# Which engine compares the token numbers in the expert stage of a hybrid decoder step

## The reference

```
pg = softmax(x @ w_rg); g_top = argmax(pg); pg_top = max(pg)          # 4 groups
fl = (x @ w_re) of the 4 experts in group g_top; pf = softmax(fl)
top_p, top_i = top_k(pf, 2)
wts = top_p / sum(top_p) * pg_top;  eid = g_top * 4 + top_i           # 16 experts
act = silu(h @ w_gate[e]) * (h @ w_up[e])                             # 2048 -> 512
y   = sum over the two chosen e of wts * (act @ w_down[e])            # 512 -> 2048
x   = x + y;   result = RMSNorm(x)
```

## Time and profile before

| what | us |
|---|---|
| median of 3 runs | 1614.38 |
| lowest and highest of them | 1611.1 and 1617.32 |
| the profiled execution, its own time | 1609.06 |
| its span, from the first to the last instruction | 1607.3 |
| TensorE busy | 1386.7 (86%) |
| VectorE busy | 682.8 (42%) |
| GpSimd busy | 247.9 (15%) |
| mean granted TensorE clock | 0.931 |

### The profile page before, as it was taken

One profiled execution on the slowest core, in us unless ns is written; L12 is line 12 of the kernel. 1 busy time (PEld: TensorE's weight loads), 2 busy tenths in 40 slices (PEclk: granted clock), 3 DMA queues, 4 the chain that ended last, 5 costly groups with the idle time before them and its releaser, 6 DMA issues. The chain is left out here.

```text
span 1607.3 us, 27516 instructions
## 1 busy us (share of the span) xinstructions
PE 1386.7 (86%) x10524; PEld 857.5 (53%) x10524; DVE 682.8 (42%) x1199; ACT 330.3 (21%) x734; POOL 247.9 (15%) x176
## 2 busy tenths in 40 slices
PE   7999999998999798778999899587889878887554
PEld 4478887777888566544544664433334333333221
DVE  3154333433553455574100223525455545654225
ACT  3001001222433244474000222111011111111102
POOL 0000000003000000000000000055344534453230
PEclk9999999999998699798999999789899989998877
DMA  9244547434430477104932234788958899859995
GB/s 346 104 171 168 188 146 259 149 120 171 172 112 7 144 233 233 47 1 172 310 111 105 96 114 187 298 321 367 377 245 326 353 421 375 367 191 418 421 422 217
DMA packets 108676, 360.96 MB, mean 225 GB/s; under 512 B 16462, under 2 KB 44150, under 8 KB 80290
## 3 DMA queue, kind: packets, MB, share of 16 engines
q1 hardware_dynamic: 104866, 329.63, 53.9%
q0 software_dynamic: 3232, 22.16, 3.8%
q10 hardware_dynamic: 512, 8.26, 1.4%
HBM read 482.68 MB, written 17.05 MB: 311 GB/s over the span
## 5 line engine op out<-in xcount | busy, mean ns | idle before, releaser
L2509 PE MATMUL bank<-ring,hT_e 128*32 128x256 f32 x3328 | 220.2, 415 | 87.6 <-DMA ring<-in_w_exp_up 50.1
L2597 DVE TENSOR_TENSOR x<-x,bank 128x1024 f32<-128x1024 f32 x156 | 183.1, 1215 | 262.8 <-PE bank L2496 256.7
L2465 POOL COPY ring<-ring 128x2048 f32 x104 | 194.9, 1902 | 246.8 <-DMA ring<-in_w_exp_gate 236.8
L2509 PEld LDWEIGHTS bank<-ring,hT_e 128*32 128x32 f32 x3328 | 113.2, 117 | 217.9 <-issue 168.9
L1853 PE MATMUL bank<-W,mixT 128*128 128x512 f32 x256 | 112.7, 600 | 1.6 <-DVE mixT L2088 1.6
L2525 PE MATMUL bank<-W,const 128*32 128x512 f32 x832 | 95.8, 596 | 13.1 <-ACT const L2555 11.2
L2496 PE MATMUL bank<-const,own_rows 32*128 32x512 f32 (+1 forms) x600 | 92.2, 685 | 6.7 <-DVE x L2597 6.7
L1853 PEld LDWEIGHTS bank<-W,mixT 128*128 128x128 f32 x256 | 48.9, 193 | 63.0 <-issue 60.8
L2551 ACT ACTIVATE gate<-bank 64x256 f32<-64x256 f32 x26 | 9.8, 376 | 321.9 <-PE bank L2509 321.9
L1833 POOL MEMSET mix<- 128x1024 f32 x1 | 1.0, 952 | 453.9 <-PE bank L1845 453.9
L517 PE MATMUL bank<-raw,hT 128*128 128x256 f32 (+1 forms) x288 | 65.2, 384 | 0.0
(11 more groups left out here) (424 smaller groups left out, 2069.7 us busy)
## 6 DMA issues: line engine op xcount, KB each, us to landing
ring<-in_w_exp_gate SPq DMA_DIRECT2D x108, 1024.0 KB
ring<-in_w_exp_up SPq DMA_DIRECT2D x104, 1024.0 KB
W<-in_w_exp_down SPq DMA_DIRECT2D x104, 1024.0 KB
raw<-in_w_in SPq DMA_DIRECT2D x10, 2048.0 KB
raw<-in_w_in SPq DMA_DIRECT2D x8, 2096.0 KB
W<-in_w_out SPq DMA_DIRECT2D x3, 4096.0 KB, 13.5
k_in<-in_cache_sel_k SPq DMA_DIRECT2D x64, 128.0 KB, 2.3
v_in<-in_cache_sel_v SPq DMA_DIRECT2D x64, 128.0 KB, 3.4
```

The costliest lines, as they stand in the source:

```text
L2465: pool.tensor_copy(w_g[:, quarter(q), :], held[:, quarter(q), :]).then_inc(g_copied[q], 1)
L2509: mm = pe.matmul(GATE[lane, 0:256], hT[:, k, q, :], (w_g if n < 2 else w_u)[:, c, cols], start=(c == 0), stop=(c == KC - 1))
L2597: ins = dve.tensor_tensor(x[rows, r, cols], x[rows, r, cols], src[rows, :], ALU.add)
```

## The change

GpSimd makes `own_rows` instead of VectorE. `find_rows` moves to GpSimd's loop, behind the gather and ahead of the copy of gate quarter 2 (the third). It is now two instructions: a copy of the unit's column of `token_of` into a new one-column tile `row_token`, and the comparison with that column. A semaphore (`token_picked`) stands between them. Ahead of them GpSimd waits until the moves of the unit before are done (`moved`); that count starts at 3, so the waits of VectorE's `add` are raised by 3. A further semaphore (`token_ready`) tells GpSimd once that the token numbers are written. After the loop the last two units are written out: quarters 0 and 1, `find_rows`, quarters 2 and 3, `find_rows`. TensorE's code stays.

```diff
--- before.py
+++ after.py
@@ -2376,6 +2376,7 @@
             hT = side("hT_e", [P, 4, 4, UNIT])
             gate = side("gate", [P, FF // 2])
             from_row = side("from_row", [P, 1], I32)
+            row_token = side("row_token", [P, 1])
             token_no = side("token_no", [P, UNITS_EACH, UNIT])
             own_rows = side("own_rows", [P, TOK])
             UP = slice(P // 2, P)
@@ -2387,7 +2388,7 @@
                 sem("e_" + n) for n in ("pe_passed", "slot_ready", "h_turned", "h_copied", "silu_ready", "act_ready", "a_turned", "a_copied",
                                         "y_copied"))
             gathered = sem("e_gathered")
-            own_ready, moved, added, own_moved, summed = (sem("e_" + n) for n in ("own_ready", "moved", "added", "own_moved", "summed"))
+            own_ready, token_ready, token_picked, moved, added, own_moved, summed = (sem("e_" + n) for n in ("own_ready", "token_ready", "token_picked", "moved", "added", "own_moved", "summed"))
             junk = w_d[:, 0, :]
             ms = side("f_ms", [P, TILES])
             squared, scaled, rooted, ready, stored = (sem("f_" + n) for n in ("squared", "scaled", "rooted", "ready", "stored"))
@@ -2464,19 +2465,35 @@
                                 pool.wait_ge(gu_used[q], turn)
                             pool.tensor_copy(w_g[:, quarter(q), :], held[:, quarter(q), :]).then_inc(g_copied[q], 1)
 
+                    def find_rows(turn):
+                        pool.tensor_copy(row_token[:, :], token_of[:, bass.ds(turn, 1)]).then_inc(token_picked, 1)
+                        pool.wait_ge(token_picked, turn + 1)
+                        pool.sem_inc(pool_passed, 1)
+                        pool.tensor_scalar(own_rows[:, :], token_no[:, :, :].rearrange("p k j -> p (k j)"), row_token[:, 0:1], None,
+                                           ALU.is_equal).then_inc(own_ready, 1)
+
                     expert_of = lambda turn: pool.value_load(experts[0:1, bass.ds(turn, 1)], min_val=0, max_val=NE - 1)
                     before_last = count(pool, 2)
                     gather(0)
                     copy_gate(0, range(4), expert_of(0), later=False)
                     pool.wait_ge(h_turned, 1)
                     gather(1)
+                    pool.wait_ge(token_ready, 1)
+                    pool.sem_inc(moved, 3)
                     with pool.Fori(0, before_last) as turn:
                         e = expert_of(turn + 1)
                         copy_gate(turn + 1, (0, 1), e)
                         pool.wait_ge(h_turned, turn + 2)
                         gather(turn + 2)
+                        pool.wait_ge(moved, turn * 3 + 3)
+                        find_rows(turn)
                         copy_gate(turn + 1, (2, 3), e)
-                    copy_gate(before_last + 1, range(4), expert_of(before_last + 1))
+                    copy_gate(before_last + 1, (0, 1), expert_of(before_last + 1))
+                    pool.wait_ge(moved, before_last * 3 + 3)
+                    find_rows(before_last)
+                    copy_gate(before_last + 1, (2, 3), expert_of(before_last + 1))
+                    pool.wait_ge(moved, before_last * 3 + 6)
+                    find_rows(before_last + 1)
 
                 @block.tensor
                 def _(pe):
@@ -2586,10 +2603,6 @@
                                                  scalar=row_w[UP, bass.ds(turn, 1)], in1=gate[UP, :],
                                                  op0=ALU.mult, op1=ALU.mult).then_inc(act_ready, 1)
 
-                    def find_rows(turn):
-                        dve.tensor_scalar(own_rows[:, :], token_no[:, :, :].rearrange("p k j -> p (k j)"), token_of[:, bass.ds(turn, 1)], None,
-                                          ALU.is_equal).then_inc(own_ready, 1)
-
                     def add_tile(r, banks):
                         rows = slice(0, TILE_ROWS[r])
                         for h, src in enumerate(banks):
@@ -2598,16 +2611,16 @@
                         return ins
 
                     def add(turn, r):
-                        dve.wait_ge(moved, turn * 3 + r + 1)
+                        dve.wait_ge(moved, turn * 3 + r + 4)
                         add_tile(r, bank2[0:2]).then_inc(added, 1)
 
                     dve.tensor_copy(token_no[:, 0, :], cst("slot_no")[:, 0:UNIT])
                     own.link(dve.tensor_tensor(token_no[:, 1:, :], cst("slot_no")[:, 0:UNIT].unsqueeze(1).to_broadcast([P, UNITS_EACH - 1, UNIT]),
                                                cst("tile_over")[:, 1:].unsqueeze(2).to_broadcast([P, UNITS_EACH - 1, UNIT]), ALU.add))
                     dve.sem_inc(added, 3)
+                    dve.sem_inc(token_ready, 1)
                     drain(0)
                     activate(0)
-                    find_rows(0)
                     drain(1)
                     add(0, 0)
                     add(0, 1)
@@ -2615,13 +2628,11 @@
                     with dve.Fori(1, last) as turn:
                         activate(turn)
                         add(turn - 1, 2)
-                        find_rows(turn)
                         drain(turn + 1)
                         add(turn, 0)
                         add(turn, 1)
                     activate(last)
                     add(last - 1, 2)
-                    find_rows(last)
 
                     def add_last(k):
                         dve.wait_ge(own_moved, k + 1)
```

## The result

The changed kernel takes 1634.38 us at the median of 4 runs (1631.17 to 1638.5), the kernel before on the same chip 1614.49. The ratio is 1.0125, with a 95% interval from 1.0095 to 1.0156: slower by 20 us. The forecast of 1618 was too low, and the time lies 4 us above the range. The profiled execution took 1631.17 us (span 1629.4, mean granted clock 0.924). L2472 is now the comparison on GpSimd, L2513 the move, L2526 gate and up, L2542 the down projection.

The account below looks back on a forecast made before the run. Expert stage: weight loads bound its end from 1437, set by when loads after 1435 begin. Load order +0.6, unit 19's clock +1.1 and five experts' clock +1.6 made +3.3 us on the 1614.38 median: 1618, range 1608 to 1630.

Parts of the forecast that it names:

- the margin of the loads: In five experts before unit 19, the last up load could come 3.6 us later free; excess 0.9, counted as +1.6 us.
- Rival 2: Each new wait breaks the load chain: +9.7 us, 1624; decided by quarters freed over 3.6 us later; chance 0.23.
- The new wait: In an expert's second units TensorE waits for GpSimd's comparison behind the next gate landing: 2.5 to 4.4 us, eight times.
- The clock: After such waits TensorE falls to half clock in seven of ten cases, 1.6 us each: +1.1 at unit 19, +1.6 before.
- The comparison on GpSimd: Added per unit on GpSimd: comparison 0.60 us, column copy and semaphore 1.04, together 1.64 us.
- Rival 3: GpSimd compares slowly: 1620 at 1.9 us, 1627 at 3.2, 1631 at 3.8; chance 0.12.
- The removed stalls: VectorE's ten comparison collisions go; their 38 us of unit time lie mostly off the path, only unit 19's touching it.
- rival 1: The stalls pay: with a cheap comparison and the clock kept up, about -6 us, hence 1608; chance 0.17.
- The collision: VectorE's slow comparison beside GpSimd's gather and gate copies, up to 4.51 us in ten of 26 units, would go.
- rival 4: The collision stays on VectorE with hT or the adds as victim: 1622; chance 0.03.
- Unit 7's carry and unit 19: Unit 7's +1.7 us reaches unit 18 as -0.8 (possibly to +1.7); with unit 19's delay the sum is +0.6 us.
- Loads after 1435 starting within 3 us of now: Sign of being right: the last experts' weight loads, issued after 1435, start at most 3 us from their present time.

Follow-up runs that it names:

- e_none: The kernel before without the comparison in units 1 to 25 (own_rows keeps unit 0's result): 1606.97 us, ratio 0.9955.
- e_swap: The kernel before with VectorE making hT ahead of the comparison: 1605.29 us, ratio 0.9944.
- e_accum: The kernel before with VectorE's comparison in the form that also sums its result, the sum unused: 1606.65 us, ratio 0.9949.
- e_early: The changed kernel with GpSimd comparing at the start of its turn into a second buffer, which ScalarE copies into own_rows: 1606.57 us, ratio 0.9959.
- e_narrow: The changed kernel with GpSimd comparing only the first 32 of 320 token numbers: 1631.93 us, ratio 1.0123.
- e_ungate: The changed kernel with an inner GpSimd loop meant to wait for the newest gate load only for a new expert; the wait stayed: 1641.62 us, ratio 1.0176.
- e_best2: e_accum with gate copies waiting for the newest gate load only if the expert is new, else the one before: 1599.88 us, ratio 0.9912.

## Why the prediction was wrong, point by point

- **The failed step** is the margin of the loads, in the part on the clock: "the last could come 7.5 - 3.9 = 3.6 us later at no cost", of which five experts' excess of 0.9 was then counted half, and with a chance of 0.7. (The 3.9 is worked out nowhere; with the 4.29 named just before it the margin would be 3.2.) That step assumes that a longer second unit hides beside the loads. It doesn't: in the changed kernel TensorE waits for an up load in units 4, 14 and 22 to 25 alone, so from unit 5 to 13 and from 15 to 21 what a second unit takes longer moves the units behind it. Where a wait for an up load does follow, it takes in 2 us at most: it is 9.93 us in e_none and 7.93 in the changed kernel at unit 4, 9.75 and 7.79 at unit 14, and 9.68 and 9.67 at unit 22, where the load comes as much later as TensorE does. I had asked when the last up quarter is needed, and not what else moves with it: in unit 2's case the first down load and the first of the next expert's up loads started 4.7 us later too. The sum gave the loads +1.6 us; from e_none, which has neither comparison nor collision, to the changed kernel the stage grows by 27.0 us, and the 7 to 9 us that the removed stalls were worth come off. Rival 2 is the nearest: its point of decision was named (3.6 us later), and its price, +9.7, was half of what came, since it counted five experts and their excess over the margin. I gave it 0.23.
- **The new wait** was sized well: eight waits, in the eight units named, 2.6 to 4.3 us long where 2.5 to 4.4 had been worked out, 4.29 at unit 7 for some 4.1.
- **The clock** was mis-sized. I took 1.6 us in seven of ten cases. In the changed kernel A has 137.9 - 30.3 of waits - 8 x 10.87 of work at the full clock = 20.6 us, 2.6 a unit; in e_none the same sum is 100.8 - 7.5 - 87.0 = 6.3. So 14 us of slow matmuls stand beside 23 us of extra waiting. They aren't spread evenly: some 1.7 us in each of units 7, 12, 17 and 19, near the 1.6 of the prediction, and 3.1 to 4.2 in units 2, 5, 10 and 15.
- **The comparison on GpSimd** takes 1.09 us, not 0.60, while the column copy and its semaphore take 0.19 + 0.28 (1198.18 to 1198.64) and not 1.04. From the end of the gather to the end of the comparison it is 1.57 us where 1.64 stood: the sum was right by two errors that cancel. Rival 3 is out, and with it the 3.2 us estimated from the 12 cycles an element in the GPSIMD Engine Reference of the Trainium skill (section "Elementwise — side-by-side cycle accounting"): 1.09 us for 320 elements is a third of it.
- **The removed stalls.** "Mostly not on the path" was right in direction: 38 us of unit time were worth 7 to 9 us (e_none, e_swap, e_accum). I had put the gain of the last one only, and 0.17 on rival 1 at -6, which is near their price. e_early, where GpSimd compares and nobody waits, brought it.
- **The collision** is gone, and free units are 15.82 us apart where "near 15.8" stood: rival 4 is out.
- **Unit 7's carry and unit 19**, -0.8 to +1.7 and +0.6 in the sum, were lost among the other six. "Loads after 1435 starting within 3 us of now" failed: they start 21.5 us later.

Open: what the price of a microsecond of wait is made of, between the clock and the loads' order, was not separated by a kernel that has one without the other; why e_narrow's up load at unit 14 is waited for longer; and what makes e_ungate slower than the changed kernel.

## What to carry to other kernels

An operation that is moved to an idle engine takes the place in that engine's queue, with all that the queue waits for there: look for the longest wait just ahead of the new place, and for who reads what stands behind it. When loads are issued in one fixed order as their buffers come free, a delay of the last user can pass to the loads queued behind it; ask for the whole queue, not for the first transfer, and ask in which units the engine waits for a load at all. And if a wait is in the way, see whether it waits for the right thing: a count that also runs on for data not needed yet cost 6 to 7 us in a kernel without the collision (e_best2 against e_accum), about what the collision itself did, and 34 in the changed one.

## What the runs showed of the hardware

- The comparison of 128x320 against one column a lane takes 0.37 us on VectorE alone, up to 4.51 beside a gather and two gate copies on GpSimd, 1.09 on GpSimd, and 0.53 on VectorE in the form that also sums, which was never slow (0.546 at most in 26, in e_accum).
- On GpSimd a comparison of 128x32 took 0.37 us and one of 128x320 took 1.09: 0.72 for 288 more columns, which leaves some 0.29 for the rest, an estimate.
- A loop on GpSimd with a count of 0 in a register ran its body once, in both kernels that tried it.
- In one and the same unit a shorter idle time of TensorE was followed by more time at half clock: the work behind it took 5.94 us after 4.29 idle (changed kernel, unit 7), 7.22 after 3.58 (e_narrow), and 4.30 in a free unit. Over all eight second units together the kernel with the shorter waits lost 1.1 us less to it.
